# Two mixer layers of a one-core kernel: one c-gate tile read earlier, up projections and branch tiles spread over four PSUM banks, h scaled tile by tile, one slot's halves moved

## The chip, the cores and the metric

The kernel runs on one core of a Trainium2 chip. The metric is the device time of one execution in microseconds, the median of several runs. All arithmetic is in fp32, or in fp32r for the matmuls.

## The reference

The first block (meta tokens, window and forgetting attention, gated feed-forward) is not touched by the change. Its output, 512 tokens by 1024 channels, goes through two layers of this form:

```python
def hybrid_layer(x, c_act, cos, sin, w_ada, b_ada, w_in, ...):
    shift, scale, gate = jnp.split(c_act @ w_ada + b_ada, 3, axis=-1)
    u = x * (1.0 + scale[:, None, :]) + shift[:, None, :]
    proj = jnp.einsum("bsd,dp->bsp", u, w_in)
    a_in, a_gate, b_in, b_gate, q_lat, kv_lat, k_rope, c_gate, merge_logits = jnp.split(proj, ...)
    a1, a2 = jnp.split(a_in, 2, axis=-1)
    a = causal_depthwise_conv(a1 * jax.nn.sigmoid(a2), conv_a_w) + conv_a_b      # 31 taps
    y_a = (jax.nn.silu(layer_norm(a, ln_a_g, ln_a_b)) * jax.nn.silu(a_gate)) @ w_a_out
    xb, gb, gc = jnp.split(b_in, 3, axis=-1)
    y_b = (gb * causal_depthwise_conv(gc * xb, conv_b_w) * jax.nn.silu(b_gate)) @ w_b_out  # 3 taps
    q = rms_norm_2(q_lat, q_norm_g) @ w_uq          # 8 heads, 64 + 32 rotated
    kv = rms_norm_2(kv_lat, kv_norm_g) @ w_ukv      # keys and values
    o = causal_block_attention(q, k, v)
    y_c = (o * jax.nn.silu(c_gate)) @ w_c_out
    g_a, g_b, g_c = jnp.split(jax.nn.sigmoid(merge_logits), 3, axis=-1)
    m = g_a * y_a + g_b * y_b + g_c * y_c
    return layer_norm(DEEPNORM_ALPHA * x + gate * (m @ w_o), ln_g, ln_b)
```

## The kernel before

Activations lie transposed: channels on the 128 partitions, the 512 tokens along the free axis, so that a channel tile is 128x512. Weights come as a stream of slots of 128x2048 numbers (1 MB), three of them in SBUF (`NBUF`). Each fp32 product is made of three fp32r matmuls (`mm3`, lines 603 to 605): high half by high half, high by low, low by high. So every slot goes through four steps: SyncE loads it (line 481, after the slot three before it is done), ScalarE rounds it to its high half (`slot_hi`, in the layers `next_hi`), VectorE subtracts to get the low half (`slot_lo`, `next_lo`), and TensorE waits for that half (`split_ready`). Every activation that is to be multiplied is split in the same way: `hi` on ScalarE, `rest` on VectorE.

Each engine has its own hand-written program, and each engine takes its instructions in order; semaphores join them. What the change touches is in the loop over the two layers (`L`). In a layer the slots are, in order: three of latents (`L_LAT`), two of the c gate (`L_CG`), two of the query up projection (`L_UQ`), one of the key and value up projection (`L_UKV`), six of branch a (`L_A`) between the pieces of the attention heads, eight of branch b (`L_B`), eighteen of merge (`L_M`: logits in pairs of slots followed by a slot of a branch's output projection, `y_slot`; twice for branch c, twice for b, then four slots of logits and two of branch a's output) and four of the output projection (`L_WO`). A slot of 48 matmuls takes some 11 us; it fills two PSUM tiles of 24 matmuls each, or in `L_UQ`, `L_UKV` and `y_slot` four or eight smaller tiles.

PSUM: result tiles alternate between bank 0 and bank 1. Reads of a tile by ScalarE or VectorE count up `bank_read[0]` or `bank_read[1]`; `wait_fill(fills, b)` on TensorE waits until every tile of that parity is read, and a new tile is written only then. Banks 2 to 5 hold latents early in a layer and attention scores later, and stand unused in the merge stage. Bank 6 (`B_O`) and 7 (`B_ST`) hold attention outputs and the sums of squares.

The orders around the change, per layer:

- ScalarE after the latents: `root` for the query norm, high halves of three latent tiles, a copy of the rotated key (`krope`), then SiLU of both tiles of the first c-gate slot into `cg`, then `root(nsum + 1)` for the key norm, two more latent halves, the high half of slot `L_CG + 2` (the first of `L_UQ`), and the other two `cg` tiles. VectorE's reciprocal of R (`inv_root`, line 1670), the latent products and the low half of that same slot follow the second `root`.
- VectorE in the attention: after the softmax of head `hd` it waits for slot `L_A + hd` and makes a tile of `ain`, and then, for heads 2, 4 and 6, `gate_c` for the pair of heads before. TensorE waits for that product (`t_ready`) before it writes the next outputs into bank 6.
- ScalarE at the end of branch b: eight scalings of `h` in a row, then `gates` of the merge stage, the first thing in which is the high half of the next slot.
- Merge slots 12 to 15: `gates(s)` first makes the high half of the next slot, then reads the two tiles. Between s == 1 and s == 2 stand the root, VectorE's reciprocal and four multiplications of `cacc`, and four SiLUs on ScalarE.

Of the kernel before, what the change touches and what calls it, by code (L numbers as in the profile page):

```python
# [23 lines left out]
P = 128  # L24
# [169 lines left out]
def program(nc, a, out):  # L194
    ctx = ExitStack()
    with ctx:
# [172 lines left out]
        LAT_BANK = (2, 3, 4, 5, 0, 6)  # L369

# [223 lines left out]
        def _(pe):  # L594
            def wait_fill(fills, b):

                v = fills.f[b].val()
                if not (isinstance(v, int) and v == 0):
                    pe.wait_ge(bank_read[b], v)
                fills.take(b)  # L600
# [421 lines left out]
            for L in range(LAYERS):  # L1022
# [23 lines left out]
                for s in range(2):  # L1046
# [4 lines left out]
                    for j in range(4):  # L1051
                        wait_fill(fills, j % 2)
                        for k in range(3):
                            whi, wlo = w(g, k * 4 * P + j * P)
                            last = mm3(bank(j % 2), whi, wlo, lat_h[:, k, :], lat_l[:, k, :], k == 0, k == 2)
# [5 lines left out]
                for j in range(4):  # L1061
                    wait_fill(fills, j % 2)
                    for k in range(2):
                        whi, wlo = w(g, k * 4 * P + j * P)
                        last = mm3(bank(j % 2), whi, wlo, lat_h[:, 3 + k, :], lat_l[:, 3 + k, :], k == 0, k == 1)
                    last.then_inc(tile_full, 1)
                for t in range(NB):
                    wait_fill(fills, t % 2)
                    for k in range(2):
                        whi, wlo = w(g, D + k * T, T)  # L1070
                        last = mm3(bank(t % 2), lat_h[:, 3 + k, t * P:(t + 1) * P], lat_l[:, 3 + k, t * P:(t + 1) * P],
# [5 lines left out]
                for b in range(2):  # L1077
                    pe.wait_ge(bank_read[b], fills.f[b].val())
# [38 lines left out]
                def y_slot(s, yh, yl, ready):  # L1117

                    split_ready(G + s)
                    for j in range(4):  # L1120
                        wait_fill(fills, j % 2)
                        for k in range(KC):
# [3 lines left out]
                            last = mm3(bank(j % 2), whi, wlo, yh[:, k, :], yl[:, k, :], k == 0, k == KC - 1)  # L1126
# [12 lines left out]
                for s in range(2):  # L1139
                    y_slot(L_M + 16 + s, ya_h, ya_l, KD + 5 + 3 * KC)  # L1140
# [43 lines left out]
        def _(sc):  # L1184
# [264 lines left out]
            for L in range(LAYERS):  # L1449
# [24 lines left out]
                root(nsum)  # L1474
                for j in range(3):
# [5 lines left out]
                for j in range(2):  # L1481
                    full(tf, G + L_CG, j == 1)
                    act_(cg[:, j, :], bank(j), ACT.Silu).then_inc(bank_read[j], 1)
# [13 lines left out]
                for j in range(4):  # L1497
                    full(tf, G + L_UKV, False)
                    for e in range(2):
                        last = act_(K[0:DH, 2 * j + e, :], bank(j % 2, T, DH * e, DH * (e + 1)), ACT.Copy,  # L1500
# [3 lines left out]
                for t in range(NB):  # L1504
                    full(tf, G + L_UKV, t == NB - 1)
                    act_(Vc[:, t, :], bank(t % 2), ACT.Copy).then_inc(bank_read[t % 2], 1)
# [47 lines left out]
                for j in range(KD):  # L1554
# [7 lines left out]
                def gates(s, dst, q0):  # L1562
                    next_hi(s + 1)
# [4 lines left out]
                for br in range(2):  # L1568
                    for half in range(2):
                        s = L_M + 6 * br + 3 * half  # L1570
                        gates(s, gt, 0)
                        gates(s + 1, gt, 2)
                        next_hi(s + 3)
# [832 lines left out]
```

## Time and profile before

| | us |
|---|---|
| median of 3 runs (lowest to highest) | 1867.81 (1864.39 to 1869.49) |
| the profiled execution | 1867.15 |
| its span, first to last instruction | 1865.2 |
| TensorE busy | 1783.6 (96%) |
| VectorE busy | 1062.8 (57%) |
| ScalarE busy | 689.0 (37%) |
| GpSimd busy | 117.1 (6%) |

In the profile PE is TensorE's matmuls, PEld its weight loads, DVE is VectorE, ACT is ScalarE, POOL is GpSimd and SP is SyncE. L603 and the like are lines of the kernel. Most operations go through small helpers, so L1186 is any ScalarE activation, L1626 any VectorE tensor-tensor operation, and the tile names tell them apart. Matmuls are pipelined: one is shown as busy for 0.39 us, but the next starts 0.23 us after it. The first layer runs from about 731 to 1284 us of the span, the second from there to the end.

### The profile page before, as it was taken

What the parts mean: (1) busy time and instruction counts of PE and PEld (TensorE: products, weight loads), DVE (VectorE), ACT (ScalarE), POOL (GpSimd) and SP (SyncE); (2) the same over time, 40 slices, a digit from 0 to 9 for tenths busy, and PEclk for the clock granted to TensorE, in tenths of its full rate; (3) what the DMA queues carried; (4) which work ended last, traced back from release to release, by engine and by line L of the source; (5) the groups of instructions that cost most, each with busy time, mean ns of one, the idle gap of its engine ahead of it and who ended that gap; (6) DMA issues with size and microseconds to landing.
All of it is one profiled execution on the core that took longest, in us unless ns stands there. A gap on an engine that the chain in (4) does not pass through costs nothing.

```text
span 1865.2 us, 20425 instructions
## 1 busy us (share of the span) xinstructions
PE 1783.6 (96%) x8186; PEld 1425.2 (76%) x8186; DVE 1062.8 (57%) x1724; ACT 689.0 (37%) x1056; POOL 117.1 (6%) x120
## 2 busy tenths in 40 slices
PE   8999998999999999999899999999999999999996
PEld 7766766788888887777788788777777778788775
DVE  6344443776665336634368766557543458766555
ACT  4425454422222234464423322532455422322432
POOL 2100001011000000100000000021100000000002
PEclk8999999999999999999999999999999999999998
DMA  4220012265554321211122222221321112222221
GB/s 163 106 102 24 23 46 82 85 208 204 200 181 164 130 91 68 90 69 68 46 90 91 90 91 103 78 90 46 113 91 49 65 68 91 90 91 90 91 90 46
DMA packets 29532, 177.40 MB, mean 95 GB/s; under 512 B 3613, under 2 KB 3757, under 8 KB 12286
## 3 DMA queue, kind: packets, MB, share of 16 engines
q1 hardware_dynamic: 20448, 144.71, 21.6%
q0 software_dynamic: 8608, 31.21, 4.8%
q8 instruction: 64, 1.05, 0.2%
q10 hardware_dynamic: 382, 0.19, 0.0%
q14 instruction: 30, 0.25, 0.0%
HBM read 171.28 MB, written 4.78 MB: 94 GB/s over the span
## 4 chain that ended last, share of the span: by engine, by line
PE 72%; DVE 6%; ACT 3%; issue 1%; POOL 1%; DMA 0%; DVEq 0%; POOLq 0%
PE ps L603 22%; PE ps L605 22%; PE ps L604 22%; PE ps L1106 2%; PE ps L1091 2%; DVE w_lo L1626 2%; DVE h L1626 1%; PE ps L1097 1%; DVE R L1670 1%; ACT w_hi L1186 1%; POOL acc L524 1%; ACT h L1186 1%; DVE cacc L1633 1%; DVE tmp L1626 0%; DVE ps L2024 0%
## 5 line engine op out<-in xcount | busy, mean ns | idle before, releaser
L603 PE MATMUL ps<-Xh,w_hi 128*128 128x512 f32 (+1 forms) x1664 | 657.0, 395 | 23.8 <-DVE w_lo L1626 9.3
L604 PE MATMUL ps<-Xl,w_hi 128*128 128x512 f32 (+1 forms) x1664 | 642.5, 386 | 0.0
L605 PE MATMUL ps<-Xh,w_lo 128*128 128x512 f32 (+1 forms) x1664 | 642.4, 386 | 0.0
L1626 DVE TENSOR_TENSOR w_lo<-w_raw,w_hi 128x2048 fp32r<-128x2048 f32 (+1 forms) x161 | 312.4, 1942 | 348.8 <-ACT w_hi L1186 348.8
L603 PEld LDWEIGHTS ps<-Xh,w_hi 128*128 128x128 f32 x1664 | 315.4, 190 | 99.2 <-issue 24.4
L1186 ACT ACTIVATE w_hi<-w_raw 128x2048 fp32r<-128x2048 f32 (+1 forms) x155 | 259.7, 1678 | 304.8 <-DMA w_raw<-in_w 278.6
L604 PEld LDWEIGHTS ps<-Xl,w_hi 128*128 128x128 f32 x1664 | 315.7, 190 | 65.3 <-issue 4.8
L605 PEld LDWEIGHTS ps<-Xh,w_lo 128*128 128x128 f32 x1664 | 315.4, 190 | 63.2
L1633 DVE SCALAR_TENSOR_TENSOR cacc<-ain,vec,cacc 128x512 f32<-128x512 f32 x240 | 161.9, 748 | 0.0
L1186 ACT ACTIVATE gt<-ps 128x512 f32<-128x512 f32 x48 | 28.2, 597 | 205.4 <-PE ps L605 205.3
L605 PE MATMUL ps<-act_h,w_lo 128*128 128x512 f32 x176 | 70.2, 399 | 0.0
L604 PE MATMUL ps<-act_l,w_hi 128*128 128x512 f32 x176 | 69.4, 394 | 0.0
L603 PE MATMUL ps<-act_h,w_hi 128*128 128x512 f32 x176 | 69.0, 392 | 0.0
L1186 ACT ACT_TABLE_LOAD x52 | 66.7, 1283 | 3.9 <-issue 3.0
L1186 ACT ACTIVATE Pc<-ps,nmax 128x128 f32<-128x128 f32 (+1 forms) x64 | 33.8, 528 | 60.7 <-DVE nmax L2024 59.6
L1885 DVE CUSTOM_DVE_ANT_0 ada_prod<-ada_w,cact 128x1024 f32<-128x1024 f32 x44 | 53.8, 1223 | 0.1
L1186 ACT ACTIVATE btmp<-ps 128x512 f32<-128x512 f32 x16 | 9.6, 600 | 119.0 <-PE ps L605 119.0
L1106 PE MATMUL ps<-PTc,Vc 128*64 128x128 f32 x320 | 42.6, 293 | 5.7 <-DVE tmp L1626 2.9
L1106 PEld LDWEIGHTS ps<-PTc,Vc 128*64 128x64 f32 x320 | 38.8, 149 | 11.0 <-issue 7.3
L2024 DVE CUSTOM_DVE_ANT_0 ps<-ps,mask 128x128 f32<-128x128 f32 (+1 forms) x64 | 31.4, 499 | 25.5 <-PE ps L1091 24.8
L1186 ACT ACTIVATE Pr<-ps,nmax 128x144 f32<-128x144 f32 (+1 forms) x64 | 31.1, 491 | 39.8 <-DVE nmax L1799 39.8
L1626 DVE TENSOR_TENSOR ain<-sq,ps 128x512 f32<-128x512 f32 x8 | 5.5, 688 | 65.2 <-PE ps L605 65.2
(306 smaller groups left out, 2158.9 us busy)
## 6 DMA issues: line engine op xcount, KB each, us to landing
w_raw<-in_w SPq DMA_DIRECT2D x134, 1024.0 KB, 4.8
ada_w<-in_w_ada POOLq DMA_DIRECT2D x48, 512.0 KB, 4.7
bias_scratch<-brow POOLq DMA_DIRECT2D x2, 1312.0 KB, 6.4
h<-in_xT SPq DMA_DIRECT2D x4, 512.0 KB, 5.7
out<-h SPq DMA_DIRECT2D x4, 512.0 KB, 2.6
bias<-bias_scratch POOLq DMA_DIRECT2D x1, 1024.0 KB, 6.8
bias<-bias_scratch POOLq DMA_DIRECT2D x1, 512.0 KB, 5.0
cact<-in_c POOLq DMA_DIRECT2D x1, 512.0 KB, 6.8
```

What stands on the lines that cost most here:

```text
L524: nc.gpsimd.tensor_tensor(acc[:, :], acc[:, :], src, ALU.add).then_inc(sq_added, 1)
L603: nc.tensor.matmul(o_, whi, xhi, start=start, stop=False)
L604: nc.tensor.matmul(o_, whi, xlo, start=False, stop=False)
L605: return nc.tensor.matmul(o_, wlo, xhi, start=False, stop=stop)
L1091: nc.tensor.matmul(bank(2 + b, P * (b + 1)), Q[:, hd, b * P:(b + 1) * P], K[:, hd, 0:P * (b + 1)], start=True, stop=True).then_inc(s2_full, 1)
L1097: last = nc.tensor.transpose(bank(2 + b, P, c0=P * k), Pc[:, P * (tri(b) + k):P * (tri(b) + k + 1)], ident[:, :])
L1106: last = nc.tensor.matmul(bank(B_O, P, DH * (hd % 2), DH * (hd % 2 + 1), c0=P * b), Vc[:, k, DH * hd:DH * (hd + 1)], PTc[:, P * (tri(b) + ...
L1186: return nc.scalar.activation(o_, i_, f, **kw)
L1626: return nc.vector.tensor_tensor(o_, a_, b_, op)
L1633: return nc.vector.scalar_tensor_tensor(o_, a_, s_, b_, op0, op1)
L1885: nc.vector.tensor_tensor_reduce(prod, ada_w[:, par, :], cact[:, :], 1.0, 0.0, ALU.mult, ALU.add, ada_sum[:, par:par + 1]).then_inc(ada_do ...
L2024: nc.vector.tensor_tensor_reduce(bank(2 + b, n), bank(2 + b, n), mask[:, NM + 384 - P * b:NM + 384 + P], 1.0, 3e38, ALU.add, ALU.min, nmax ...
```

## The change

In both layers:

1. ScalarE reads the first c-gate tile (bank 0) right after the first `root`, ahead of the three latent high halves. The second stays where it was.
2. The up projections and the branch output tiles go to four banks: tile j into `bank(j)` in place of `bank(j % 2)`; the four value tiles go to banks 4, 5, 0 and 1 (`VC_BANK`). `wait_fill` gets a `lag`: with 1 it leaves the newest tile of that parity out of the wait. The wait ahead of the first scores leaves out the last two value tiles.
3. `gate_c` stands ahead of the wait for the a slot, not behind it.
4. The eight scalings of `h` are called one by one, each behind a `gates` of the merge stage.
5. The high and low halves of merge slot 15 are made at s == 1: on ScalarE behind the root and ahead of the four SiLUs, on VectorE behind the reciprocal and ahead of the four multiplications of `cacc`.

The diff, cut to its core:

```diff
@@ -367,6 +367,7 @@
...
         LAT_BANK = (2, 3, 4, 5, 0, 6)
+        VC_BANK = (4, 5, 0, 1)
@@ -592,9 +593,9 @@
...
         def _(pe):
-            def wait_fill(fills, b):
-
-                v = fills.f[b].val()
+            def wait_fill(fills, b, lag=0):
+
+                v = fills.f[b].val(-lag)
                 if not (isinstance(v, int) and v == 0):
@@ -1049,33 +1050,33 @@
...
                     for j in range(4):
-                        wait_fill(fills, j % 2)
+                        wait_fill(fills, j % 2, 0 if s == 0 and j < 2 else 1)
                         for k in range(3):
                             whi, wlo = w(g, k * 4 * P + j * P)
-                            last = mm3(bank(j % 2), whi, wlo, lat_h[:, k, :], lat_l[:, k, :], k == 0, k == 2)
+                            last = mm3(bank(j), whi, wlo, lat_h[:, k, :], lat_l[:, k, :], k == 0, k == 2)
                         last.then_inc(slot_done if j == 3 else tile_full, 1)
...
                 for j in range(4):
-                    wait_fill(fills, j % 2)
+                    wait_fill(fills, j % 2, 0 if j < 2 else 1)
                     for k in range(2):
                         whi, wlo = w(g, k * 4 * P + j * P)
-                        last = mm3(bank(j % 2), whi, wlo, lat_h[:, 3 + k, :], lat_l[:, 3 + k, :], k == 0, k == 1)
+                        last = mm3(bank(j), whi, wlo, lat_h[:, 3 + k, :], lat_l[:, 3 + k, :], k == 0, k == 1)
                     last.then_inc(tile_full, 1)
                 for t in range(NB):
-                    wait_fill(fills, t % 2)
+                    wait_fill(fills, t % 2, 1)
                     for k in range(2):
                         whi, wlo = w(g, D + k * T, T)
-                        last = mm3(bank(t % 2), lat_h[:, 3 + k, t * P:(t + 1) * P], lat_l[:, 3 + k, t * P:(t + 1) * P],
+                        last = mm3(bank(VC_BANK[t]), lat_h[:, 3 + k, t * P:(t + 1) * P], lat_l[:, 3 + k, t * P:(t + 1) * P],
                                    whi, wlo, k == 0, k == 1)
...
                 for b in range(2):
-                    pe.wait_ge(bank_read[b], fills.f[b].val())
+                    pe.wait_ge(bank_read[b], fills.f[b].val(-1))
                 pe.wait_ge(kpe_spread, L + 1)
@@ -1114,16 +1115,16 @@
...
-                def y_slot(s, yh, yl, ready):
+                def y_slot(s, yh, yl, ready, follows=False):
...
                     for j in range(4):
-                        wait_fill(fills, j % 2)
+                        wait_fill(fills, j % 2, 1 if follows or j >= 2 else 0)
                         for k in range(KC):
...
                             whi, wlo = w(G + s, k * 4 * P + j * P)
-                            last = mm3(bank(j % 2), whi, wlo, yh[:, k, :], yl[:, k, :], k == 0, k == KC - 1)
+                            last = mm3(bank(j), whi, wlo, yh[:, k, :], yl[:, k, :], k == 0, k == KC - 1)
                         last.then_inc(slot_done if j == 3 else tile_full, 1)
@@ -1137,7 +1138,7 @@
...
                 for s in range(2):
-                    y_slot(L_M + 16 + s, ya_h, ya_l, KD + 5 + 3 * KC)
+                    y_slot(L_M + 16 + s, ya_h, ya_l, KD + 5 + 3 * KC, s == 1)
@@ -1472,15 +1473,16 @@
...
                 root(nsum)
+                full(tf, G + L_CG, False)
+                act_(cg[:, 0, :], bank(0), ACT.Silu).then_inc(bank_read[0], 1)
                 for j in range(3):
...
-                for j in range(2):
-                    full(tf, G + L_CG, j == 1)
-                    act_(cg[:, j, :], bank(j), ACT.Silu).then_inc(bank_read[j], 1)
+                full(tf, G + L_CG, True)
+                act_(cg[:, 1, :], bank(1), ACT.Silu).then_inc(bank_read[1], 1)
                 root(nsum + 1)
@@ -1497,13 +1499,13 @@
...
                     for e in range(2):
-                        last = act_(K[0:DH, 2 * j + e, :], bank(j % 2, T, DH * e, DH * (e + 1)), ACT.Copy,
+                        last = act_(K[0:DH, 2 * j + e, :], bank(j, T, DH * e, DH * (e + 1)), ACT.Copy,
                                     scale=-MLA_SCALE)
...
                     full(tf, G + L_UKV, t == NB - 1)
-                    act_(Vc[:, t, :], bank(t % 2), ACT.Copy).then_inc(bank_read[t % 2], 1)
+                    act_(Vc[:, t, :], bank(VC_BANK[t]), ACT.Copy).then_inc(bank_read[t % 2], 1)
@@ -1551,7 +1553,7 @@
...
-                for j in range(KD):
+                def scale_h(j):
                     if L == 0:
@@ -1559,8 +1561,9 @@
...
-                def gates(s, dst, q0):
-                    next_hi(s + 1)
+                def gates(s, dst, q0, ahead=False):
+                    if not ahead:
+                        next_hi(s + 1)
                     for j in range(2):
@@ -1569,17 +1572,20 @@
...
                         gates(s, gt, 0)
+                        scale_h(4 * br + 2 * half)
                         gates(s + 1, gt, 2)
+                        scale_h(4 * br + 2 * half + 1)
                         next_hi(s + 3)
...
                 for s in range(4):
-                    gates(L_M + 12 + s, gt if s < 2 else gt2, 2 * (s % 2))
+                    gates(L_M + 12 + s, gt if s < 2 else gt2, 2 * (s % 2), s == 2)
                     if s == 0:
...
                         root(nsum + 3, 1)
+                        next_hi(L_M + 15)
                         for t in range(KC):
@@ -2005,7 +2011,7 @@
...
                         full(tf, G + (L_UQ + s), j == 3)
-                        tt(Q[:, 4 * s + j, :], bank(j % 2), rope_q[:, :], ALU.mult).then_inc(bank_read[j % 2], 1)
+                        tt(Q[:, 4 * s + j, :], bank(j), rope_q[:, :], ALU.mult).then_inc(bank_read[j % 2], 1)
                         bf.take(j % 2)
@@ -2044,6 +2050,8 @@
...
                         norm2(hd, b)
+                    if hd and hd % 2 == 0:
+                        gate_c(hd // 2 - 1)
                     if hd < 4:
@@ -2054,8 +2062,6 @@
...
                         bf.take(1)
-                    if hd and hd % 2 == 0:
-                        gate_c(hd // 2 - 1)
                 gate_c(3)
@@ -2115,9 +2121,9 @@
...
                         if br == 0:
-                            tt(mj, g_[:, j, :], bank(j % 2), ALU.mult).then_inc(bank_read[j % 2], 1)
+                            tt(mj, g_[:, j, :], bank(j), ALU.mult).then_inc(bank_read[j % 2], 1)
                         else:
-                            tt(tmp[:, j % 2, :], g_[:, j, :], bank(j % 2), ALU.mult).then_inc(bank_read[j % 2], 1)
+                            tt(tmp[:, j % 2, :], g_[:, j, :], bank(j), ALU.mult).then_inc(bank_read[j % 2], 1)
                             ve.wait_ge(bank_read[j % 2], bf.f[j % 2].val())
@@ -2143,7 +2149,8 @@
...
                 for s in range(4):
-                    next_lo(L_M + 13 + s)
+                    if s != 2:
+                        next_lo(L_M + 13 + s)
                     tf.add(1)
@@ -2156,6 +2163,7 @@
...
                         inv_root(nsum + 3)
+                        next_lo(L_M + 15)
                         for t in range(KC):
```

## Rows read from the trace of the kernel before

**Rows 1.** The page: busy time by engine, and the granted clock in 40 slices.

```profile
PE 1783.6 (96%) x8186; PEld 1425.2 (76%) x8186; DVE 1062.8 (57%) x1724; ACT 689.0 (37%) x1056; POOL 117.1 (6%) x120
...
PEclk8999999999999999999999999999999999999998
```

**Rows 2.** Waits of TensorE, whole span: total us, times, longest us.

```profile
PE ps L603 <- DVE w_lo L1626: 9.3, 4, 3.2
...
PE ps L603 <- ACT cg L1186: 5.6, 2, 2.8
...
PE ps L603 <- DVE tmp L1626: 3.6, 3, 1.4
...
PE ps L1106 <- DVE tmp L1626: 2.9, 2, 1.5
PE ps L603 <- DVE Q L1626: 2.8, 2, 1.4
```

**Rows 3.** Timeline of PE, c gate: start, duration (us), instruction, [idle before].

```profile
743.65 1.02 PE L641 MATMUL ps<-acc,ones 128*128 128x512 f32 x2
...
744.74 0.40 PE L604 MATMUL ps<-Xl,w_hi 128*128 128x512 f32 x1
...
760.87 1.02 PE L641 MATMUL ps<-acc,ones 128*128 128x512 f32 x2
764.68 0.47 PE L603 MATMUL ps<-Xh,w_hi 128*128 128x512 f32 x1 [2.78 <-ACT cg L1186]
...
768.86 0.39 PE L605 MATMUL ps<-Xh,w_lo 128*128 128x512 f32 x1
...
777.28 0.40 PE L603 MATMUL ps<-lat_h,w_hi 128*128 128x512 f32 x1
...
1346.37 0.40 PE L603 MATMUL ps<-lat_h,w_hi 128*128 128x512 f32 x1
```

**Rows 4.** Timeline of ACT and DVE in the same stretches.

```profile
759.16 1.29 ACT L1186 ACTIVATE lat_h<-tmp 128x512 fp32r<-128x512 f32 x2 [10.27 <-DVE tmp L1633]
...
762.64 1.28 ACT L1186 ACT_TABLE_LOAD   x1
763.94 1.08 ACT L1186 ACTIVATE cg<-ps 128x512 f32<-128x512 f32 x2
...
766.34 0.69 ACT L1186 ACTIVATE R<-ps,eps 128x512 f32<-128x512 f32 x1
...
774.43 2.29 DVE L1626 TENSOR_TENSOR w_lo<-w_raw,w_hi 128x2048 fp32r<-128x2048 f32 x1 [1.19 <-ACT w_hi L1186]
...
1342.25 2.29 DVE L1626 TENSOR_TENSOR w_lo<-w_raw,w_hi 128x2048 fp32r<-128x2048 f32 x1 [1.19 <-ACT w_hi L1186]
```

**Rows 5.** Timeline of ACT, DVE and PE where h is scaled, both layers.

```profile
1021.20 4.26 ACT L1186 ACTIVATE h<-h 128x512 f32<-128x512 f32 x8
...
1027.37 2.29 DVE L1626 TENSOR_TENSOR w_lo<-w_raw,w_hi 128x2048 fp32r<-128x2048 f32 x1 [1.56 <-ACT w_hi L1186]
...
1029.71 0.50 PE L603 MATMUL ps<-Xh,w_hi 128*128 128x512 f32 x1 [1.71 <-DVE w_lo L1626]
...
1599.04 2.29 DVE L1626 TENSOR_TENSOR w_lo<-w_raw,w_hi 128x2048 fp32r<-128x2048 f32 x1 [3.04 <-ACT w_hi L1186]
...
1601.39 0.70 PE L603 MATMUL ps<-Xh,w_hi 128*128 128x512 f32 x1 [3.18 <-DVE w_lo L1626]
```

**Rows 6.** Timeline of ACT and PE ahead of merge slot 15, first layer.

```profile
1184.14 1.90 ACT L1186 ACTIVATE w_hi<-w_raw 128x2048 fp32r<-128x2048 f32 x1
...
1187.35 1.08 ACT L1186 ACTIVATE gt<-ps 128x512 f32<-128x512 f32 x2
...
1188.49 0.79 PE L603 MATMUL ps<-Xh,w_hi 128*128 128x512 f32 x1 [2.19 <-DVE w_lo L1626]
```

**Rows 7.** Timeline of PE within the first branch-c slot.

```profile
1046.10 0.40 PE L605 MATMUL ps<-yc_h,w_lo 128*128 128x512 f32 x1
1046.55 0.50 PE L603 MATMUL ps<-yc_h,w_hi 128*128 128x512 f32 x1
```

## The prediction

> **What bounds the kernel.** I read the page first: TensorE is busy for 96% of the span and no other engine for more than 57%, so time can only be won where TensorE stands still or runs at a lower clock [rows 1]. Then the waits of TensorE: the entries with a few long waits, not many short ones, are the ones that an order of work can cure. Five kinds matter: w_lo (9.3 us in 4), cg (5.6 in 2), tmp ahead of matmuls (3.6 in 3), tmp ahead of L1106, the attention outputs (2.9 in 2), and Q (2.8 in 2); nearly all come once or twice per layer [rows 2]. Last, the timeline around each, to see what is late next.
>
> **How a wait is priced.** A steady matmul starts 0.228 us after the one before (768.86 to 777.28 is 37 of them), but is drawn 0.39 long, so an idle time of x costs x + 0.16 [rows 3]. After a longer wait the clock falls from its 2.4 GHz level to the 1.2 GHz one: from 764.68 to 768.86 11 intervals take 4.18 us in place of 2.50, so such a dip costs 1.68 more. It came after idle times of 2.78, 2.19 and 3.18 us (first matmul drawn 0.79 and 0.70 long in the last two), not after 1.71 [rows 3, 5, 6]. Where it starts is partly chance.
>
> **1. The c-gate tile read ahead.** The wait of 2.78 goes: ScalarE sits idle for 10.27 us ahead of the latent halves, and tile 0 is full some 5 us before them, so a table load of 1.28 and a SiLU of 0.6 fit in; the added wait has the three halves, krope and the second root queued behind it and delays none. If that cover were gone, the halves would slip by up to 1.9 us, and the first up projection wants them only 10 us later [rows 3, 4]. Unhindered, the up projection would start at 760.87 + 1.09 (as 743.65 to 744.74) + 47 x 0.228 = 772.66, 4.6 us ahead of 777.28 [rows 3]. But it waits for its own slot's low half, which VectorE ends at 774.43 + 2.29 = 776.72, at the end of the chain second root, reciprocal, latent products, high half [rows 4]. That chain moves with the root alone: before, a table load, two SiLUs and a table load stand behind krope, and R starts at 766.34; now one SiLU (0.6), then the load (1.28): R at 762.64 + 0.60 + 1.28 + 0.04 = 764.56, 1.78 earlier. So the low half ends at 774.94 and the up projection starts at 775.00: **2.3 us won, and a new wait of 2.2 idle**, as long as the one that brought a dip in rows 6. In the second layer the low half ends at 1342.25 + 2.29 - 1.78 = 1342.76 and the projection starts at 1342.8 in place of 1346.37, 3.6 won (the old dip was longer there), again behind an idle time of about 2.2. I take a dip at both: 2.3 + 3.6 - 2 x 1.6 = **2.7 us**; bounds 2.7 and 5.9.
>
> The table load row shows 1.28 us with 0.02 before the next activation [rows 4]. The Trainium skill (ScalarE: Activation LUTs, "What ACT_TABLE_LOAD costs") adds a drain of some 1.38 us to each switch of set; no row here shows it. By the page the root would come 3.2 us earlier in place of 1.78, the new wait would shrink to 0.8 and item 1 would be worth 8.7 us; the sum stays with the rows.
>
> **2. Four banks.** The Q wait (1.4 idle, 1.56 us) comes from VectorE, which makes the next low half before it reads Q tile 0; with four banks TensorE writes two more tiles first, 4.2 us, and by then the reads are through: 1.56 per layer. Two of the three tmp waits are those of the second branch-a slot, the same pattern, 1.4 idle: 1.56 per layer [rows 2]. Half-hidden waits go too, such as 1046.10 to 1046.55, 0.45 in place of 0.23, and the first matmul after it 0.1 slow [rows 7]; there are some seven per layer, most of them of 0.15, together 0.8 to 1.2. I take 1.1. The relaxed wait ahead of the first scores frees up to 0.9 us, but the first softmax chain hangs on the last value tile through ScalarE, and TensorE meets it at the transposes: zero. Sum 2 x (1.56 + 1.56 + 1.1) = **8.4 us**; bounds 6 and 10.
>
> **3. gate_c earlier.** 1.45 idle per layer [rows 2]: bank 6 has long been full, so the product is made right behind the softmax. VectorE then waits in `rest` for ScalarE's high half, which stands behind the PTc copies; queued behind it is the ain tile, which is not due until the slot ends 4 us later. **3.1 us**; bounds 2.5 and 3.2.
>
> **4. h scaled tile by tile.** Eight scalings (4.26 us) stand ahead of the high half of slot L_M + 1; VectorE idles 1.56 for it. With them gone it starts 1.56 earlier, bound then by its own convolution taps: matmul at 1029.71 - 1.56, of the 1.87 lost. In the second layer 3.04, and the dip goes, as the wait left is 0.2 [rows 5]: 1.55 + 3.04 + 1.6 = **6.2 us**; bounds 4.6 and 6.9. Each scaling (0.5 to 0.7) now delays one later high half; those are ready 5 us or more before use, so nothing on the path. If the scaling made ScalarE reload its table, that would be 2.6 more per slot of 11, still hidden.
>
> **5. Halves of slot 15 moved.** TensorE waits for w_lo until 1188.49 (about 2.35 lost, and a dip) [rows 6]. w_lo comes 5 us earlier now. But slot 15's first tile goes into bank 0, where slot 14's first tile waits to be read by a Sigmoid that ScalarE takes only after the four SiLUs. These start 2.2 us later (VectorE's low half of 2.29 now precedes the multiplications that feed them), and the high half of 1.90 no longer follows them: the Sigmoid ends at 1187.35 + 0.60 + 2.2 - 1.9 = 1188.25, TensorE starts at 1188.3. **0.2 per layer, 0.4 us**; the wait changes its name from w_lo to gt and keeps its dip. Bounds -0.6 (the Sigmoid a little later than w_lo was) and 8.2 (waits and dips gone).
>
> **The sum** is 2.7 + 8.4 + 3.1 + 6.2 + 0.4 = 20.8 us: span 1865.2 to 1844.4, profiled run 1867.15 to 1846.4; that run stood 0.66 under the median 1867.81, so the median goes to **1847.0 us**.
>
> **Rivals.**
> A. *No dips at the new waits.* The waits of 2.0 to 2.2 us at the up projections and slot 15 leave the clock at 2.4 GHz. Four times 1.6 more: 27.2 won, 1840.6. For it: 1.71 brought none. Against: 2.19 did. Chance 0.25.
> B. *More low clock.* In attention or behind the new waits some four more dips appear, as the whole order shifts in time; 20.8 - 4 x 1.68 = 14.1, 1853.7. Chance 0.12.
> C. *Nothing takes the place of anything.* My readings in 1 and 5 are wrong, and the whole idle time and its dips go: 5.9 + 2 x 2.35 = 10.6 in item 1 in place of 2.7, 8.2 in item 5 in place of 0.4: 36.5 won, 1831.3. It needs another order on ScalarE than the text of the kernel has. Chance 0.05.
> D. *The change hardly does what it says.* Each wait returns as the next one (low halves behind VectorE's queue, which has only 0.2 to 0.3 us spare in item 4) and under 5.6 us stay: 1864. The rows speak against it, as in 2 and 3 the next in line is 1 to 4 us away. Chance 0.06.
> E. *Slower, through the clock in the four-bank stages.* Hopping over banks brings small pauses between groups, and the clock falls for part of the up projections and branch tiles: 408 matmuls per layer, 816 in all, 0.2 us each at the low level, 163 us if all. It cancels my gain from 13% of them on, and at 17% the kernel is 6.9 us slower, 1874.7. Against it: matmul groups there follow each other without a wait once the reads keep up, and the feed-forward stage, which already goes over four to eight banks, keeps its granted clock at nine tenths or more (slices 9 to 15) [rows 1]. Chance 0.02.
>
> This last is what the Trainium skill warns of (TensorE: Matmul & The Clock Gate, "A second HAM failure mode: psum-queue depth-cycling"): cycling through banks makes TensorE pause often enough for its clock to swing. Taken at its word the time is that of rival E.
>
> **The numbers.** My forecast has 0.50. The range 1838 to 1856 takes in A and B with the bounds of items 2 to 4, and leaves out C, D and E, 0.13. A difference of 0.3%, 5.6 us, is about what a measurement of this kernel can tell from none. Faster by more: forecast, A, B and C, 0.92; within: D, 0.06; slower: E, 0.02.
>
> **What would show it.** Item 1: no wait for cg, R 1.8 us earlier behind krope, and a wait of TensorE for w_lo at the first lat_h matmul. Item 2: no wait for Q and none for tmp at the second branch-a slot. Item 3: none for tmp ahead of L1106. Item 4: w_lo waits at the start of the merge stage at 0.3 us or less. Item 5: the wait of some 2 us stays, now for ScalarE's gt. The prediction is wrong if the waits of 1 or 5 are absent (C) or if stretches of the low clock come where no wait is (B, E).

## The result and the profile after

The changed kernel takes **1845.62 us** (median of 4 runs, 1843.48 to 1847.28) against 1866.74 for the kernel before in the same measurement: ratio 0.9886, interval 0.9868 to 0.9904, 21.1 us less. The forecast was 1847.0 in a range of 1838 to 1856. The profiled execution took 1847.28, its span 1845.3. Rows of the page, as in [rows 1]:

```profile
span 1845.3 us, 20425 instructions
...
PE 1775.6 (96%) x8186; PEld 1423.1 (77%) x8186; DVE 1061.9 (58%) x1724; ACT 688.3 (37%) x1056; POOL 123.7 (7%) x120
...
PEclk8899999999999999999999999999999999999998
```

The work is the same to the instruction; what went is idle time and low clock. The waits of TensorE over the whole span, as in [rows 2]:

```profile
PE ps L1098 <- DVE Pc L1636: 8.3, 16, 0.7
PE ps L604 <- DVE Xl L1632: 6.1, 5, 2.6
PE ps L604 <- ACT gt L1187: 4.5, 2, 2.2
PE ps L604 <- DVE w_lo L1632: 4.4, 2, 2.2
...
PE ps L604 <- DVE tmp L1632: 0.8, 1, 0.8
```

Of the five kinds that were read before, cg, Q and the tmp ahead of the attention outputs are gone, tmp ahead of matmuls is down from three to the one outside the layers (at 365.5 us), and w_lo is down from four to two. Those two are new ones at the up projections, and gt is a new name. One of the five Xl waits has grown, from 1.87 to 2.57 us: it stands once, at the start of the second layer.

Where the time went, from the starts of the first matmul of each stage (timeline of PE), both layers added:

| stretch | before | after | won | forecast |
|---|---|---|---|---|
| second sum of squares to up projection | 34.09 | 28.29 | 5.80 | 5.9 |
| up projection to first scores | 61.80 | 59.32 | 2.48 | 3.1 less 3.2 for two dips |
| first scores to first branch-c slot | 469.30 | 463.33 | 5.97 | 3.1 + 6.2 |
| the branch-c and branch-b part of the merge | 243.47 | 242.17 | 1.30 | 2.2 (half-hidden waits, here and in row 2) |
| slots 14 and 15, to the first branch-a slot | 53.49 | 50.38 | 3.11 | 0.4 |
| from the first branch-a slot to the next sum of squares | 100.65 | 97.08 | 3.57 | 3.1 |

That is 22.2 us (forecast 20.8). The first layer began 2.16 us later in this execution than in the one of before (first sum at 745.81, not 743.65 as in [rows 3]), in a part whose work is the same in both kernels, and 0.2 is spread over the rest: 19.9 less in the spans, 21.1 in the medians.

Timeline of ACT, DVE and PE where the c gate was, as in [rows 3, 4]:

```profile
764.83 0.60 ACT L1187 ACTIVATE cg<-ps 128x512 f32<-128x512 f32 x1
765.44 1.28 ACT L1187 ACT_TABLE_LOAD   x1
766.74 0.69 ACT L1187 ACTIVATE R<-ps,eps 128x512 f32<-128x512 f32 x1
...
774.84 2.29 DVE L1632 TENSOR_TENSOR w_lo<-w_raw,w_hi 128x2048 fp32r<-128x2048 f32 x1 [1.19 <-ACT w_hi L1187]
...
777.19 0.51 PE L604 MATMUL ps<-lat_h,w_hi 128*128 128x512 f32 x1 [2.20 <-DVE w_lo L1632]
...
778.25 0.63 PE L604 MATMUL ps<-lat_h,w_hi 128*128 128x512 f32 x1
...
1336.22 0.51 PE L604 MATMUL ps<-lat_h,w_hi 128*128 128x512 f32 x1 [2.20 <-DVE w_lo L1632]
```

Only one SiLU and one table load stand ahead of R. The low half ends at 774.84 + 2.29 = 777.13, and TensorE starts 0.06 later: the wait that was forecast, of the forecast length. The first matmul is drawn at 0.51 and those from 778.25 on at 0.63: the clock fell behind the wait, in both layers.

Windows of PE: stretch, its length, busy time of each engine, granted clock, DMA share, GB/s. First the new wait's aftermath, then the rest of the query projections, the first branch-c slots, and slot 15:

```profile
777.00:782.00 5.00, 4.81 (x14) 3.81 (x15) 3.07 (x3) 3.85 (x3) 0.00 (x0) 0.66 0.42 175
782.00:800.00 18.00, 18.00 (x79) 14.49 (x78) 9.33 (x11) 4.29 (x5) 0.00 (x0) 1.00 0.31 117
1048.00:1058.00 10.00, 10.00 (x46) 8.20 (x44) 8.23 (x11) 0.60 (x1) 0.00 (x0) 1.00 0.27 107
...
1185.40:1190.00 4.60, 4.58 (x20) 3.81 (x21) 3.52 (x6) 2.94 (x6) 0.00 (x0) 1.00 0.40 169
```

The four-bank stages run at 1.00 of the 2.4 GHz level once the wait's dip is over (rows 2 and 3). Slot 15 (last row) has no dip, though its wait is still there:

```profile
1173.34 0.69 ACT L1187 ACTIVATE R<-ps,eps 128x512 f32<-128x512 f32 x1
1173.92 1.91 ACT L1187 ACTIVATE w_hi<-w_raw 128x2048 fp32r<-128x2048 f32 x1
...
1180.43 2.94 ACT L1187 ACTIVATE cacc<-cacc,vec 128x512 f32<-128x512 f32 x4 [3.30 <-DVE cacc L1632]
1183.38 1.28 ACT L1187 ACT_TABLE_LOAD   x1
1184.68 1.08 ACT L1187 ACTIVATE gt<-ps 128x512 f32<-128x512 f32 x2
...
1185.42 0.47 PE L604 MATMUL ps<-Xh,w_hi 128*128 128x512 f32 x1 [2.25 <-ACT gt L1187]
```

The high half comes right behind R, but the Sigmoid that frees bank 0 stands behind four SiLUs, a table load and VectorE's multiplications, so TensorE waits 2.25 us for it where it waited 2.19 for w_lo [rows 6].

Where h is scaled, the first matmul of the merge stage follows its low half with a wait too small to be named (0.21 us lost, 0.22 in the second layer, in place of the waits of 1.71 and 3.18 in [rows 5]), and one scaling stands behind a pair of gates:

```profile
1024.96 2.29 DVE L1632 TENSOR_TENSOR w_lo<-w_raw,w_hi 128x2048 fp32r<-128x2048 f32 x1
...
1027.30 0.50 PE L604 MATMUL ps<-Xh,w_hi 128*128 128x512 f32 x1
...
1027.78 0.62 ACT L1187 ACTIVATE h<-h 128x512 f32<-128x512 f32 x1
```

### The profile page after: what moved, and what is told of

It reads as the page before. It is cut to its first block, busy times and chain, and to the rows that moved or that the text cites. A ratio compares the mean times of both kernels' runs of the same rounds, so it can differ in the third digit from the quotient of the medians.

```text
span 1845.3 us, 20425 instructions
## 1 busy us (share of the span) xinstructions
PE 1775.6 (96%) x8186; PEld 1423.1 (77%) x8186; DVE 1061.9 (58%) x1724; ACT 688.3 (37%) x1056; POOL 123.7 (7%) x120
## 4 chain that ended last, share of the span: by engine, by line
PE 72%; DVE 7%; ACT 2%; issue 1%; POOL 1%; DVEq 0%; POOLq 0%
PE ps L604 22%; PE ps L606 22%; PE ps L605 22%; PE ps L1107 2%; PE ps L1092 1%; DVE w_lo L1632 1%; DVE R L1676 1%; DVE h L1632 1%; PE ps L1098 1%; POOL acc L525 1%; DVE ps L2030 1%; ACT w_hi L1187 1%; DVE tmp L1639 0%; DVE cacc L1639 0%; ACT cacc L1187 0%
## 5 line engine op out<-in xcount | busy, mean ns | idle before, releaser
L521 POOL TENSOR_TENSOR acc<-cacc 128x512 f32<-128x512 f32 x2 | 9.5, 4752 | 526.0 <-DVE cacc L1639 526.0
```

## The experiments

Three questions: does each item bring what its own sum says, are the two waits that remain what I say they are, and what decides whether a wait costs a dip. Ratios are to the kernel before on the same chip, with their 95% interval. A difference of 0.3% is about 5.6 us, more than most single items bring, so each item was timed over 10 to 12 runs, and the timeline of one profiled execution says where its gain lies.

### Each item alone

The edits are the hunks of the diff above that belong to one item, put on the kernel before: the second `full`/`act_` pair moved (item 1); `bank(j)`, `VC_BANK` and the lags (item 2); `gate_c` moved (item 3); `scale_h` (item 4); `ahead`, `next_hi(L_M + 15)` and its low half (item 5).

> The kernel before with item 1 alone (the first c-gate tile read ahead). My theory: the wait for cg (2.8 us) goes, the second root comes 1.8 us earlier, and a wait of 2.2 us for the low half of the first up-projection slot stands at the first lat_h matmul in both layers. The up projection starts 2.3 us earlier in the first layer, 3.6 in the second; with a clock dip behind the new wait in both, 2.7 us are won in all, 5.9 without dips. Rival (nothing takes the place of the wait): the up projection starts 4.6 and 5.9 us earlier, 10.6 won, and no wait for w_lo there.

> The kernel before with item 2 alone (up projections and branch tiles over four banks). My theory: 8.4 us won (6 to 10): no wait for Q, none for tmp at the second branch-a slot, and the half-hidden waits of 0.15 gone; the scores start 0.9 us earlier but the first transposes wait that much more. Rival (hopping over banks lets the clock fall): stretches at the low clock in the up projections and branch slots where no wait stands, slower than before if over 5% of these 816 matmuls run at the low level (8.4 / 163).

> The kernel before with item 3 alone (gate_c ahead of the wait for the a slot). My theory: the wait of 1.47 us ahead of the attention outputs goes in both layers and nothing else changes: 3.1 us won (2.5 to 3.2). Rival (VectorE, now waiting in rest for ScalarE's high half, makes the ain tile or the next low half late): a wait of TensorE for w_lo or sq appears at the a slots and under 1.5 us are won.

> The kernel before with item 4 alone (h scaled tile by tile). My theory: 6.2 us won: the wait at the second merge slot falls from 1.7 and 3.2 us to 0.3 or less, and the second layer's dip goes. Rival (the scalings between the Sigmoids cost ScalarE table loads and delay the high halves): more table loads than 52 in the trace, w_lo waits at later merge slots, less than 4 us won.

> The kernel before with item 5 alone (halves of merge slot 15 moved). My theory: no change, 0.4 us won (-0.6 to 0.6 apart from the chance of the dips): the wait of 2.2 us ahead of slot 15 stays in both layers and is now for ScalarE's gt. Rival (the low half was the only thing late): the wait goes, 2 x 2.35 us and two dips of 1.6 are won, about 8.

| item | ratio | 95% | won, by medians (us) | forecast |
|---|---|---|---|---|
| 1 | 0.9979 | 0.9964 to 0.9994 | 2.7 | 2.7 |
| 2 | 0.9960 | 0.9948 to 0.9972 | 7.5 | 8.4 |
| 3 | 0.9982 | 0.9970 to 0.9993 | 3.9 | 3.1 |
| 4 | 0.9980 | 0.9963 to 0.9996 | 4.9 | 6.2 |
| 5 | 0.9999 | 0.9984 to 1.0014 | 0.5 | 0.4 |

Together 19.4 us. Each interval is some 2 to 3 us wide to either side, so the agreement to a few tenths is luck. What the medians bear out is that items 1 to 4 each bring something and that item 5's gain can't be told from none. Item 2 brings 5.2 to 9.7 us, probably the most; an order of the other three is not shown.

**Item 1.** Without the other items it leaves the same wait:

```profile
772.27 0.50 PE L603 MATMUL ps<-lat_h,w_hi 128*128 128x512 f32 x1 [2.19 <-DVE w_lo L1627]
```

From the second sum to this matmul it is 14.14 us in both layers, as in the changed kernel. Where no dip followed the c-gate wait of before (item 5 alone in both layers, items 3 and 4 alone in the second), that stretch was 15.9 us, not 16.4 to 17.7: the up projection was already held by the low half, and the c-gate wait itself cost nothing there. What item 1 wins on the path is 15.91 - 14.14 = 1.77 us per layer, which is the 1.78 by which R comes earlier; the rest of my 2.3 and 3.6 was the old dip.

The old dip also made the Q wait longer. In the kernels with two banks the Q wait is 1.39 to 1.40 us in the four layers with a dip behind the c-gate wait (both of before, the first of items 3 and 4 alone) and 0.46 in the four without (both of item 5 alone, the second of items 3 and 4 alone), as here in the timeline of PE for item 5 alone:

```profile
781.79 0.50 PE L603 MATMUL ps<-lat_h,w_hi 128*128 128x512 f32 x1 [0.46 <-DVE Q L1628]
```

So items 1 and 2 overlap. From the second sum to the first scores, both layers added, the profiled execution of item 1 alone is 6.7 us shorter than that of before, that of item 2 alone 7.1, that of the whole change 8.3 (5.80 + 2.48 in the table above), and not 13.8. These are single executions, that of item 1 the fastest of its ten runs; the 2.7 of its median is not the 6.7 of this stretch.

**Item 3.** From the first scores to the first branch-c slot it is 467.84 us in place of 469.30, 1.46 won, though the clock was lower: in the two stretches of 25 us from 900 us on it was granted 0.95 and 0.91, in place of 1.00 and 0.93, so that 3.5 us of work are missing in place of 1.75. Together that is 3.2, for the 3.1 forecast.

**Item 4.** The gain at the start of the merge stage is there, but the branch-c and branch-b part gets longer: from the first branch-c to the first branch-b slot 67.35 and 67.72 us, in place of 66.48 and 66.27, and the part behind it 56.35 and 56.75 in place of 55.36. The timeline of its second layer, ACT, DVE and PE:

```profile
1675.81 0.81 ACT L1186 ACTIVATE h<-h,lnp 128x512 f32<-128x512 f32 x1
1676.52 1.91 ACT L1186 ACTIVATE w_hi<-w_raw 128x2048 fp32r<-128x2048 f32 x1
...
1678.53 2.29 DVE L1628 TENSOR_TENSOR w_lo<-w_raw,w_hi 128x2048 fp32r<-128x2048 f32 x1 [3.29 <-ACT w_hi L1186]
1680.73 0.68 DVE L1628 TENSOR_TENSOR tmp<-gt,ps 128x512 f32<-128x512 f32 x1
...
1681.47 0.50 PE L603 MATMUL ps<-yb_h,w_hi 128*128 128x512 f32 x1 [0.59 <-DVE tmp L1628]
```

The scaling delays the high half, that the low half, and that VectorE's read of branch tile 0, which on two banks TensorE needs before tile 2. The four branch slots of a layer take 0.3 to 0.5 us each more in the first layer and 0.7 in the second: 0.87 + 0.99 = 1.9 us and 1.45 + 1.39 = 2.8. With item 2 that stretch is 66.02 and 55.06, shorter than before. So the scalings are hidden by the four banks, and not by the slack I had counted. In the profiled execution that loss is made up in part by dips that did not come: the waits at slot 15 stay at 2.19 us, but the clock holds behind them in both layers (25.15 in place of 26.73 and 26.76 us), and 6.2 - 4.7 + 3.2 = 4.7. This is a sum for one execution, in which other dips came and went as well; that the medians say 4.9 does not prove it.

**Item 5.** The stretch with slots 14 and 15 is 26.79 and 26.82 us in place of 26.73 and 26.76, with a dip in both: 0.1 us lost, not 0.4 won. The 0.5 of the medians is noise.

### The two remaining waits taken away

The next two kernels, and the one with the filled wait further down, were timed beside runs of the kernel before (1863.35 us), but not beside the changed kernel. The changed kernel stood 21.1 and 23.3 us under the kernel before in its two measurements. The gate first stands 22.2 under it, the halves first 23.3, the filled wait 22.6. By their times, then, none of the three can be told from the changed kernel, and the 3.2 to 7.9 us that were expected are not seen in them. What follows is read from the stretches of the profiled executions. Only both edits together were timed beside the changed kernel.

The gate first (in `gates`, and at `s == 1` behind `next_hi(L_M + 15)`):

```diff
+                        if ahead and j == 0:
+                            continue
...
                         next_hi(L_M + 15)
+                        full(tf, G + L_M + 14, False)
+                        act_(gt2[:, 0, :], bank(0), ACT.Sigmoid).then_inc(bank_read[0], 1)
```

> The changed kernel, with slot 14's first tile read by its Sigmoid ahead of the four SiLUs (one more table load, in a stretch where ScalarE waits). If bank 0, held by the late Sigmoid, is what keeps slot 15 waiting in the changed kernel, the wait for gt (2.25 us idle, 2.4 start to start) goes in both layers: 4.8 us less than the changed kernel, and up to 3 more where a dip stood behind it. Rival (something else is late at the same moment, the slot's low half or its data): a wait of 1 us or more stays there under another name and less than 2.5 us are won.

1841.11 us, ratio 0.9877 (0.9862 to 0.9893). The Sigmoid of slot 14 now stands ahead of the SiLUs, and TensorE goes through:

```profile
1177.11 0.60 ACT L1187 ACTIVATE gt<-ps 128x512 f32<-128x512 f32 x1 [0.64 <-PE ps L606]
1177.73 1.28 ACT L1187 ACT_TABLE_LOAD   x1
...
1182.12 0.39 PE L606 MATMUL ps<-Xh,w_lo 128*128 128x512 f32 x1
1182.35 0.39 PE L604 MATMUL ps<-Xh,w_hi 128*128 128x512 f32 x1
```

The stretch to the first branch-a slot falls from 25.19 to 22.66 us in both layers: the wait was bank 0's and costs 2.5 us each time, and the two added table loads (one per layer) lie beside other work. Part of it was lost again once: at the start of the second layer TensorE waits 2.83 us for Xl, with a dip behind it. From the first matmul of the output projection to the first sum of the second layer it is 88.0 us, in place of 86.4 in the changed kernel, and 87.5 and 88.0 in the two runs with both edits. Three of the kernels with one item alone have 88.0 there too, so it is not shown that the gate is the cause.

The halves first (`next_hi(L_CG + 2)` right behind the first SiLU, its low half ahead of the second latent products):

```diff
                 act_(cg[:, 0, :], bank(0), ACT.Silu).then_inc(bank_read[0], 1)
+                next_hi(L_CG + 2)
...
-                next_hi(L_CG + 2)
...
+                next_lo(L_CG + 2)
                 latents(nsum + 1, 3, 5, V_KG)
-                next_lo(L_CG + 2)
```

> The changed kernel, with the high half of the first up-projection slot made right after the first c-gate tile, and its low half ahead of the second reciprocal. If that low half, at the end of the chain from the second root, is what took the place of the c-gate wait, the wait of 2.2 us at the first lat_h matmul goes or falls below 0.3 us in both layers: 4.7 us less than the changed kernel, and up to 3.2 more for the two dips. Rival (the low half comes together with something else, as the third c-gate tile that must be read from bank 0): a wait for cg of 1 us or more in its place, less than 2.5 us won.

1840.06 us, ratio 0.9878 (0.9861 to 0.9894). Timeline of ACT, DVE and PE:

```profile
757.54 1.91 ACT L1187 ACTIVATE w_hi<-w_raw 128x2048 fp32r<-128x2048 f32 x1
764.03 2.28 DVE L1632 TENSOR_TENSOR w_lo<-w_raw,w_hi 128x2048 fp32r<-128x2048 f32 x1
...
773.85 0.39 PE L606 MATMUL ps<-Xh,w_lo 128*128 128x512 f32 x1
774.23 0.47 PE L604 MATMUL ps<-lat_h,w_hi 128*128 128x512 f32 x1
```

The low half is ready 8 us ahead, and the up projection starts 11.94 us after the second sum in place of 14.14, 0.1 from the unhindered 47 x 0.228 + 1.09 = 11.8. Two waits of 2.2 us went, and no dip stands there in either layer.

Both edits together:

> The changed kernel with both: slot 14's first tile read ahead of the SiLUs, and the first up-projection slot's halves ahead. The two waits are in different stages, so the gains add: 9.5 us of waits and 3 to 6 of dips, 12 to 15 less than the changed kernel, some 1832. Rival (waits return downstream): less than 7.

> The changed kernel with slot 14's first tile read ahead of the SiLUs and the first up-projection slot's halves made ahead, once more beside the changed kernel: 12 us (9.5 to 15) less than the changed kernel in the same job. Rival: the difference found before came from another set of runs of the kernel before, and it is under 9.5, the two waits alone.

1831.84 us, ratio 0.9832 (0.9815 to 0.9849), and in another measurement, beside the changed kernel itself, 1832.98, ratio 0.9816 (0.9802 to 0.9831): 11.9 us under the changed kernel's 1844.84 in the same set, and the fastest version of this study. The two waits account for 4.4 + 5.0 us of it by the stretches; the rest is not traced to a place. There are two more table loads than before, and TensorE's waits have neither gt nor w_lo among the long ones:

```profile
span 1830.9 us, 20427 instructions
...
PE ps L1098 <- DVE Pc L1640: 8.4, 16, 0.7
PE ps L604 <- DVE Xl L1636: 5.2, 3, 2.8
```

### What a wait costs in clock

The wait at the up projection is left in, but filled with two fp32 matmuls per layer that nothing reads (the profile has each as two, so x4 below):

```diff
                 for s in range(2):
+                    if s == 0:
+                        keep_busy(2, bank(3), T)
                     split_ready(g)
```

> The changed kernel, with two fp32 matmuls of 128x512 into the free bank 3 ahead of the first up-projection slot: 1.8 us of work put into the new wait of 2.2, so that its idle time falls to about 0.5. If the dip there comes from TensorE's idle time, it goes in both layers with nothing else moved: 3.2 us less than the changed kernel. Rival (the dip is chance, or hangs on something other than the idle time): matmuls at the low clock stand behind the up projection's start as before, and the time is the changed kernel's within 1 us, or more by what the two matmuls overrun.

1840.78 us, ratio 0.9881 (0.9860 to 0.9902). Timeline of PE, and the window behind it:

```profile
772.20 1.88 PE L612 MATMUL ps<-mask,ident 128*128 128x512 f32 x4
774.55 0.50 PE L604 MATMUL ps<-lat_h,w_hi 128*128 128x512 f32 x1 [0.47 <-DVE w_lo L1634]
...
774.50:779.50 5.00, 4.95 (x21) 4.04 (x22) 3.06 (x3) 3.72 (x3) 0.00 (x0) 1.00 0.42 175
```

The up projection starts as late as in the changed kernel (14.14 us behind the second sum), and the clock stays at 1.00 in both layers. The stretch to the first scores is 28.1 us in place of 29.66: 1.56 us is the dip, alone. The changed kernel, run again, has both lengths in one execution: 29.66 in the first layer, with a dip, and 28.11 in the second, without.

The changed kernel itself, a second time, and with the full wait ahead of the first scores:

```diff
-                    pe.wait_ge(bank_read[b], fills.f[b].val(-1))
+                    pe.wait_ge(bank_read[b], fills.f[b].val())
```

> The changed kernel once more, on the same chip and beside the same runs of the kernel before as the three that follow: 21 us less than the kernel before, as in its first measurement (16 to 25). Its waits stand as in the first trace (2.2 for w_lo at the up projection, 2.25 for gt at slot 15). If dips behind a wait of this length are chance, they need not stand behind the same waits; if they belong to a place, both up projections have one and slot 15 none.

> The changed kernel, with the wait ahead of the first scores made full again (all four value tiles read). My theory: the relaxed wait is worth nothing, since the first softmax chain hangs on the last value tile through ScalarE: the scores start 0.9 us later per layer, the first transposes' waits (0.3 and 0.5 us, two each) shrink by as much, time within 0.5 us of the changed kernel. Rival: the relaxed wait is worth its 0.9 per layer, this kernel is 1.8 us slower.

1844.84 (ratio 0.9879, 0.9862 to 0.9897) and 1844.40 (0.9878, 0.9861 to 0.9894): no difference. The first scores start 0.9 us later with the full wait (30.55 behind the up projection in place of 29.66), and the transposes behind them run without the waits that they have in the changed kernel. Timeline of PE, first the changed kernel, then the full wait:

```profile
815.27 0.55 PE L1098 MATMUL ps<-ident,Pc 128*128 128x128 f32 x3 [0.31 <-DVE Pc L1636]
816.32 0.66 PE L1098 MATMUL ps<-ident,Pc 128*128 128x128 f32 x4 [0.50 <-DVE Pc L1636]
```

```profile
815.51 1.50 PE L1098 MATMUL ps<-ident,Pc 128*128 128x128 f32 x10
```

Counted over all 14 profiled executions, by layer (a dip is a stretch of low granted clock that begins between 0.6 us ahead of the first matmul behind the wait and 1.5 us after it):

| wait | idle, us | followed by a dip |
|---|---|---|
| w_lo at the up projection | 2.2 | 7 of 10 |
| the same, filled with matmuls | 0.5 | 0 of 2 |
| the same place, no wait (halves first) | 0 | 0 of 6 |
| cg, kernels without item 1 | 2.8 | 6 of 10 |
| w_lo at the merge stage, second layer, without item 4 | 3.2 | 4 of 5 |
| the same, first layer | 1.7 | 0 of 5 |
| slot 15, kernels without item 4 | 2.2 | 9 of 10 |
| slot 15, kernels with item 4 | 2.2 | 1 of 12 |

The count is of kernels and layers, not of repeated runs, and the cases within a row are not independent. The two filled cases alone would prove little; with the six in which the wait is gone they say that at the up projection the dip hangs on the idle time. Item 5 alone has the same wait for gt at the same length as the changed kernel, with the dip:

```profile
1188.49 0.47 PE L603 MATMUL ps<-Xh,w_hi 128*128 128x512 f32 x1 [2.25 <-ACT gt L1186]
...
1188.50:1193.00 4.50, 4.50 (x13) 3.56 (x14) 3.45 (x6) 2.84 (x6) 0.00 (x0) 0.63 0.42 178
```

So neither the length nor the name of the wait decides: 2.8 us of idle was followed by a dip less often than 2.2. What item 4 changes ahead of slot 15 that matters to the clock stays open, and so does whether it is item 4 at all: it stands alone in one kernel (0 of 2), and the other ten cases have all five items.

## Why the prediction was right, and which of its steps were not

**The total** (20.8 forecast, 21.1 measured) is right for the reason given in the main: the waits went, and those of items 1 and 5 came back under another name at nearly the same length. Rivals C (nothing takes their place, 1831.3) and D (hardly anything, 1864) are out; the new waits stand in the rows above. With both new waits taken away as well the kernel takes 1832 to 1833, near C's 1831.3.

**Item 1.** The chain of second root, reciprocal, products, high half and low half moved by 1.77 us, forecast 1.78. The two dips came as well in the profiled execution; at this place they came 7 times in 10. I had read the whole 4.6 us of idle and dip as the c gate's; it was the dip that made the difference between 15.9 and 16.4 or 17.7. The sum came out right because both readings end at the same matmul.

The R of the second root came as early as the rows had it, not 3.2 us earlier. ScalarE starts 0.02 us after its table load in the rows above, and its idle time ahead of all 52 loads is 4.0 us in total. The drain that the Trainium skill adds (ScalarE: Activation LUTs, "What ACT_TABLE_LOAD costs") is in no run here.

**Item 2.** Waits for Q and for the second branch-a slot went, 1.8 us per layer in the branch-a slots (forecast 1.56 and a share of the half-hidden ones). The relaxed wait ahead of the scores is worth zero, for the reason given: 0.9 us won, met again at the transposes. That is why the second and fourth stretches of the table together bring 1.7 more than forecast and the third as much less. The 1.56 for Q holds for a layer with the old dip only: without it the wait was 0.46, about 0.6 us of price. With item 1 in place less was left for item 2 to win there than I had added up.

**Item 3.** The wait ahead of L1106 went; 3.1 forecast, 3.9 by medians with an interval of 1.3 to 5.6 us, 3.2 by the stretch.

**Item 4: the step that failed is "so nothing on the path".** I had weighed the scalings against the time at which the high half is due at TensorE, 5 us ahead, not against what queues behind the low half on VectorE: the reads of the tiles of the slot before. It costs 4.7 us on two banks and nothing on four. In the whole change the step comes out right, by item 2, which I did not say.

**Item 5: the wait nearly as forecast, the dip not.** It stayed and took the name gt, but grew by 0.06 us where I had 0.2 less per layer; the bound of -0.6 covers that. (The upper bound of 8.2 adds up to 7.9: two waits of 2.35 and two dips of 1.6.) In the changed kernel it kept no dip in either layer, 3.2 us that I had not forecast; the stretch brings 3.1 in place of 0.4. That is half of rival A. The other way went the attention: the rows of the last heads show more low clock in the first layer than before, at the same place of the kernel.

```profile
900.00:925.00 25.00, 20.90 (x117) 15.50 (x116) 9.88 (x37) 13.23 (x34) 0.00 (x0) 1.00 0.12 43
925.00:950.00 25.00, 24.31 (x111) 20.46 (x110) 11.47 (x14) 7.84 (x7) 0.00 (x0) 0.93 0.11 43
```

```profile
900.00:925.00 25.00, 21.35 (x103) 16.04 (x101) 8.71 (x34) 10.91 (x31) 0.00 (x0) 0.86 0.12 43
925.00:950.00 25.00, 23.96 (x116) 19.95 (x117) 11.78 (x15) 8.25 (x9) 0.00 (x0) 1.00 0.12 43
```

Before (first fence), 0.07 of 25 us is missing from the clock's mean, 1.75 us of work; after, 0.14, 3.5 us. So one event of rival B, 1.75 us. With the 1.8 of the transposes that is 3.55, for the 3.3 that the third stretch fell short of its 9.3. The misses are 3.2 us in one direction and 1.75 in the other, and the first layer began 2.16 us later besides; they partly cancel, and that part of the agreement is chance.

**Rival E** did not happen. The four-bank stages run at a granted clock of 1.00 except behind the w_lo wait, with item 2 alone as with the whole change, and item 2 alone is 7.5 us faster. The pattern that the Trainium skill warns of (TensorE: Matmul & The Clock Gate, "A second HAM failure mode: psum-queue depth-cycling") needs pauses between the groups. Here two banks had them (1.40 us for Q, 1.37 at the second branch-a slot) and four banks took them away.

## What to carry to other kernels

Ask of each wait that goes what the same engine waits for next, and start the search with the second input of the same instruction: at both places where a wait came back it was a tile or a weight half that had been late all along behind the one named by the profile. Price an added instruction on an engine by everything that queues behind what it delays, tile reads on the other engine included, not by the next due time alone; and check each part for cover that another part of the same change supplies. Where the late thing is a half or a gate that could be made earlier, move that one too: two such moves were worth 11.9 us on top of this change's 21.

## What the runs showed of the hardware

A wait of 2.2 us is followed by a stretch at the 1.2 GHz level in some executions and not in others, 7 of 10 at one place, 9 of 10 or 1 of 12 at another, and costs 1.56 us when it is (28.1 against 29.66 for the same stretch). Where TensorE would have waited behind it anyway the price is lower: with two banks the same stretch is 30.87 us with the dip and 30.06 without (item 1 alone, first and second layer). A wait of 2.8 us was followed by one in 6 of 10 cases. No wait of 1.71 us or less for cg, w_lo, Q, tmp or gt in the two layers had one. Two fp32 matmuls that nothing reads, 1.88 us in the middle of the wait, kept the clock up in both layers and left the wait's end where it was.
